# A mixture-of-experts block whose weights stream through a ring: another order of the experts, one slot more

## What is computed

```
def expert_ffn(xb, w1, b1, w2, b2):
    z = xb @ w1 + b1                                   # w1: 1024 x 2048
    x_glu = jnp.minimum(z[..., ::2], SWIGLU_LIMIT)
    x_lin = jnp.clip(z[..., 1::2], -SWIGLU_LIMIT, SWIGLU_LIMIT)
    act = x_glu * jax.nn.sigmoid(SWIGLU_ALPHA * x_glu) * (x_lin + 1.0)
    return act @ w2 + b2                               # w2: 1024 x 1024

    logits = (ht @ router_w + router_b).astype(jnp.float32)
    top_vals, top_idx = lax.top_k(logits, TOP_K)       # 4 of 32
    gates = jax.nn.softmax(top_vals, axis=-1)
    ...                                                # every token through its 4 experts
    x  = x + gate2 * MoE_top4_of_32(h2)
```

## Time and profile before

| | us |
|---|---|
| runs of the kernel before | 1756.4, 1764.86, 1767.21 |
| their median | 1764.86 |
| the profiled execution | 1758.43 |
| its span, first to last instruction | 1756.7 |

### The profile page before, as it was taken

One profiled execution on the slowest core, in us unless ns is written; L12 is line 12 of the kernel. 1 busy time (PEld: TensorE's weight loads), 2 busy tenths in 40 slices (PEclk: granted clock), 3 DMA queues, 4 the chain that ended last, 5 costly groups with the idle time before them and its releaser, 6 DMA issues.

```text
span 1756.7 us, 48721 instructions
## 1 busy us (share of the span) xinstructions
PE 1481.8 (84%) x19899; PEld 832.5 (47%) x19899; DVE 776.8 (44%) x1872; ACT 302.8 (17%) x844; POOL 530.6 (30%) x532
## 2 busy tenths in 40 slices
PE   4899998689648999999898998988978978986781
PEld 2356554364335555555554545554544534542340
DVE  4857365453365444444443433433433423422225
ACT  4121265342101111111111111110101100100000
POOL 3085999108002323222232222222211212211110
PEclk9997999899868999998999999998988988987885
DMA  9442224763761704478869999999999999999997
GB/s 270 151 49 48 86 47 98 261 200 107 299 254 43 309 20 164 163 291 322 344 269 403 358 407 368 354 408 408 408 408 408 408 408 408 408 409 409 408 408 295
DMA packets 141907, 495.58 MB, mean 282 GB/s; under 512 B 20216, under 2 KB 24580, under 8 KB 137744
## 3 DMA queue, kind: packets, MB, share of 16 engines
q1 hardware_dynamic: 128960, 469.60, 70.9%
q0 software_dynamic: 8416, 19.33, 3.1%
q10 hardware_dynamic: 4432, 5.25, 0.9%
HBM read 474.18 MB, written 17.84 MB: 280 GB/s over the span
## 4 chain that ended last, share of the span: by engine, by line
PE 53%; DMA 22%; SPq 15%; DVE 5%; issue 2%; ACT 2%; POOL 0%; ACTq 0%; POOLq 0%; DVEq 0%
PE bank L1789 30%; DMA w_ring<-mlp_w 17%; SPq L422 14%; PE bank L1506 5%; PE bank L1669 3%; PE bank L1594 2%; DMA ada_slab<-ada_w 2%; PE bank L1498 2%; DMA ada_half<-ada_w 2%; PE bank L1808 1%; PE bank L1781 1%; PE bank L1603 1%; PE bank L1769 1%; DVE final_acc L1421 1%; PE bank L1698 1%
## 5 line engine op out<-in xcount | busy, mean ns | idle before, releaser
L1789 PE MATMUL bank<-w_ring,xs_T 128*32 128x256 f32 x10240 | 620.9, 394 | 67.7 <-DMA w_ring<-mlp_w 67.5
L1789 PEld LDWEIGHTS bank<-w_ring,xs_T 128*32 128x32 f32 x10240 | 330.0, 113 | 319.9 <-DMA w_ring<-mlp_w 108.6
L643 POOL DMA_INDIRECT xs<-h_rows,row_idx x82 | 189.3, 2309 | 847.7 <-DVE row_idx L1349 817.4
L1789 PE MATMUL bank<-w_ring,act_T 128*32 128x256 f32 x5120 | 338.2, 402 | 56.1 <-DMA w_ring<-mlp_w 55.9
L1789 PEld LDWEIGHTS bank<-w_ring,act_T 128*32 128x32 f32 x5120 | 154.3, 114 | 175.3 <-DMA w_ring<-mlp_w 55.7
L1367 DVE TENSOR_SCALAR glu<-bank 128x128 f32<-128x128 f32 x160 | 46.6, 291 | 402.9 <-PE bank L1789 402.9
L945 DVE TENSOR_TENSOR slot_onehot<-iota_slots,slots 128x2048 bf16<-128x2048 f32 x83 | 189.3, 2281 | 0.0
L922 ACT ACTIVATE sigmoid<-glu 128x128 f32<-128x128 f32 x160 | 48.9, 306 | 536.2 <-DVE glu L1367 466.9
L926 ACT ACTIVATE act_T<-bank 128x128 f32<-128x128 f32 x160 | 44.3, 277 | 518.1 <-PE bank L1808 518.1
L664 POOL DMA_INDIRECT ys_rows<-y_rows_sb,row_idx x80 | 82.3, 1029 | 144.2 <-DVE y_rows_sb L945 141.9
L1344 DVE TENSOR_REDUCE row_idx_f<-bank 128x1 f32<-128x2 f32 x82 | 13.0, 159 | 209.0 <-PE bank L1769 209.0
(11 more groups left out here) (336 smaller groups left out, 1534.6 us busy)
## 6 DMA issues: line engine op xcount, KB each, us to landing
w_ring<-mlp_w SPq DMA_DIRECT2D x384, 1024.0 KB
ada_half<-ada_w SPq DMA_DIRECT2D x16, 1024.0 KB, 5.0
dense_ring<-w_in SPq DMA_DIRECT2D x4, 2048.0 KB, 14.6
final_rows<-ys_rows SPq DMA_DIRECT2D x4, 2048.0 KB, 14.4
dense_ring<-ada_w SPq DMA_DIRECT2D x3, 2048.0 KB, 29.3
w_out<-w_out SPq DMA_DIRECT2D x2, 2048.0 KB, 10.6
x_all<-x SPq DMA_DIRECT2D x2, 1024.0 KB, 14.3
ada_slab<-ada_w SPq DMA_DIRECT2D x1, 2048.0 KB, 40.3
```

Of the source, the lines that this page charges most:

```text
L643: pool.indirect_dma_start(out=xs[:], out_offset=None, in_=h2_v, in_offset=bass.IndirectOffsetOnAxis(ap=idx[:, 0:1], axis=0), bounds_check= ...
L1789: last = mm(bk[BLK * j:BLK * j + BLK, 0:ZW], x(h0 + i), w[:, i, ZW * j:ZW * j + ZW], start=False, stop=(stop and i == 1))
```

## The change

```
+FIXED = 1
-SLOTS_KIB = (132, 140, 64, 72, ..., 48, 56, 148)
+SLOTS_KIB = (132, 140, 64, 72, ..., 48, 56, 148, 120)
...
             sp.wait_ge(s["x1_ready"], NT)
+            sp.wait_ge(s["blocks_ready"], 1)
+            expert = sp.value_load(eat[0:1, 1:2], min_val=0, max_val=E - 1)
             for n in range(12, 16):
-                chunk(n)
+                chunk(n, expert)
             sp.wait_ge(s["h2_tr"], NT)
             sp.wait_ge(s["h2_ready"], NT)
-            for j in range(TILES):
-                sp.dma_start(g2q[BLK * j:BLK * j + BLK], dram["mod_rows"][0, 3 * D + ZW * j:3 * D + ZW * j + ZW]
-                             .partition_broadcast(BLK)).then_inc(s["mod_loaded"], 16)
...
             for n in range(16, 21):
-                chunk(n)
+                chunk(n, expert)
             sp.wait_ge(s["blocks_ready"], 3)
+            for j in range(TILES):
+                sp.dma_start(g2q[BLK * j:BLK * j + BLK], dram["mod_rows"][0, 3 * D + ZW * j:3 * D + ZW * j + ZW]
+                             .partition_broadcast(BLK)).then_inc(s["mod_loaded"], 16)
             for n in range(21, SLOTS):
-                chunk(n)
-            expert = None
+                chunk(n, expert)
...
-                ch(tt(cmp, bc(R[7][:, 2:E], 1, n, [P, n, n]), bc(R[7][:, 2:E], 2, n, [P, n, n]), ALU.is_gt))
+                ch(tt(cmp, bc(R[7][:, FIXED:E], 1, n, [P, n, n]), bc(R[7][:, FIXED:E], 2, n, [P, n, n]), ALU.is_lt))
...
-                ch(tt(posn[:, 2:E], posn[:, 2:E], R[6][:, 2:E], ALU.min))
+                ch(tt(posn[:, FIXED:E], posn[:, FIXED:E], R[6][:, FIXED:E], ALU.min))
+                ch(tt(ordm[:], bc(posn[:], 1, E, [P, E, E]), bc(iotaE[:], 2, E, [P, E, E]), ALU.is_equal))
+                ch(tt(lessm[:], ordm[:], bc(iotaE[:], 1, E, [P, E, E]), ALU.mult))
+                ch(dve.tensor_reduce(eatf[:], lessm[:], AX.X, ALU.add))
+                dve.tensor_copy(eat[:], eatf[:]).then_inc(s["blocks_ready"], 1)
...
-            act.wait_ge(s["blocks_ready"], 2)
+            act.wait_ge(s["blocks_ready"], 3)
...
-            pe.wait_ge(s["blocks_ready"], 2)
+            pe.wait_ge(s["blocks_ready"], 3)
```

More of the change, by code:

```diff
@@ L63 @@
 W1P = 8
[L64 removed]
+SLOTS_KIB = (132, 140, 64, 72, 32, 40, 0, 8, 16, 24, 172, 180, 80, 88, 156, 164, 96, 104, 112, 48, 56, 148, 120)
 SLOTS = len(SLOTS_KIB)
@@ L210, in program @@
         rw = pack("router_w", [P, KT, E])
+        tri = pack("tri", [P, P], BF16)
+        onb = pack("ones_bf", [P, P], BF16)
+        ones = pack("ones", [P, P])
         rb = pack("router_b", [P, E])
@@ L243, in program @@
         lessm = at("order_less", 196, [P, E, E], BF16)
-        lin = at("lin", 120, [P, 2, GW])
-        actT = at("act_T", 121, [P, 2, AH, P])
-        glu = at("glu", 122, [P, 2, GW])
-        sg = at("sigmoid", 123, [P, 2, GW])
-        g2q = at("gate2_quarters", 124, [P, ZW])
+        lin = at("lin", 197, [P, 2, GW])
+        actT = at("act_T", 128, [P, 2, AH, P])
+        glu = at("glu", K0 + 0.5 + 0.0625, [P, 2, GW])
+        sg = at("sigmoid", K0 + 1.5 + 0.0625, [P, 2, GW])
+        g2q = at("gate2_quarters", 129, [P, ZW])
         bsrc = at("b_src", 172, [96, 3072])
@@ L256, in program @@
         xT = at("xs_T", 203, [P, XH, P])
-        iotab = at("iota_slots", K0 + 2.25, [P, P])
+        iotab = at("iota_slots", K0 + 2.75, [P, P])
         fing = at("final_rows", 0, [P, 16, D])
-        fx1 = at("final_x1", 172, [P, NT, D])
+        fx1 = at("final_x1", 96, [P, NT, D])
         facc = at("final_acc", 80, [P, NT, D])
@@ L459, in _ @@
                     last_block = sp.value_load(nbi[0:1, E + e:E + e + 1], min_val=0, max_val=MAXB - 1)
-                if n >= 2 * CPE and n % CPE == 0:
+                if n % CPE == 0:
                     expert = sp.value_load(eat[0:1, n // CPE:n // CPE + 1], min_val=0, max_val=E - 1)
@@ L1229, in order_positions @@
                 dve.wait_ge(s["part_mm"], 1)
-                n = E - 2
+                n = E - FIXED
                 ch(dve.tensor_scalar(R[6], bank[7][:, 6 * E:7 * E], float(E), None, ALU.mult))
@@ L1233, in order_positions @@
                 cmp = lessm[:, 0:n, 0:n]
[L1234 to L1239 removed]
+                ch(tt(cmp, bc(R[7][:, FIXED:E], 1, n, [P, n, n]), bc(R[7][:, FIXED:E], 2, n, [P, n, n]), ALU.is_lt))
+                ch(dve.tensor_reduce(R[5][:, FIXED:E], cmp, AX.X, ALU.add))
+                ch.free(dve.tensor_scalar(posn[:, FIXED:E], R[5][:, FIXED:E], 2.0, float(FIXED), ALU.mult, ALU.add))
+                ch(dve.tensor_scalar(R[6][:, FIXED:E], R[5][:, FIXED:E], -2.0, 2.0 * E - 1.0 - FIXED, ALU.mult, ALU.add))
+                ch.free(dve.tensor_copy(posn[:, 0:FIXED], iotaE[:, 0:FIXED]))
+                ch(tt(posn[:, FIXED:E], posn[:, FIXED:E], R[6][:, FIXED:E], ALU.min))
[3 more added lines that the diff above has]
+                dve.tensor_copy(eat[:], eatf[:]).then_inc(s["blocks_ready"], 1)
             def order_matrices():
[L1243 to L1244 removed]
+                ch(tt(lessm[:], bc(posn[:], 1, E, [P, E, E]), bc(posn[:], 2, E, [P, E, E]), ALU.is_lt))
             dve.wait_ge(s["norm_router_loaded"], 64)
@@ L1313, in _ @@
             dve.tensor_reduce(dslot[:], prod[:], AX.X, ALU.add).then_inc(s["blocks_ready"], 1)
-            dve.wait_ge(s["blocks_ready"], 1)
+            dve.wait_ge(s["blocks_ready"], 2)
             dve.wait_ge(s["bias_ready"], 2)
@@ L1319, in block_ends @@
                 ch.free(tt(R[2], R[4], R[0], ALU.add))
-                ch.free(tt(lessm[:], ordm[:], bc(iotaE[:], 1, E, [P, E, E]), ALU.mult))
                 ch.sync()
@@ L1481, in _ @@
                 last = tr(bank[1][:, q * DG:(q + 1) * DG], quad[:, q].rearrange("p a b -> p (a b)"), ident[0:DG, 0:DG])
-            last.then_inc(s["af_psum"], 1)
+            last.then_inc(s["pe_prep"], 1)
             early_ada(2)
```

23 lines of the change are left out of this document (5 added, 18 removed).

## The result

The changed kernel takes 1748.72 us (median of 16 runs, 1738.71 to 1757.32) where the kernel before takes 1764.76 (median of 16, 1756.4 to 1768.44). The ratio is 0.9909 [0.9887, 0.9931]: 16 us or 0.9% less. The forecast was 27.3 us less (1737.5), with a range of 1720 to 1756. So the sign was right and the size 11 us short; by the bound of 1% the change lies just inside "within 1%", the outcome to which the prediction had given 0.18.

What follows compares the result with a forecast made beforehand. PE bounds the early large-expert blocks, the weight stream the later part. Against before, the six (3,1) pairs begin 26.0 us later, take 2.6 less, and 50.8 less follows: −27.3 from 1764.86 gives 1737.5 us, range 1720 to 1756.

Steps and rivals of the forecast that it cites:

- the start: From the order to the first block: later count and a gather slowed beside chunks make it 3.0 us late, bounds 0.5 to 5.
- the seven stalls: Seven pairs of a large and a one-block expert, positions 2 to 15: 5.7 us of stall each, 39.6 together.
- the six (3,1) pairs: Pairs of a three-block and a one-block expert at the stream's pace, one chunk further ahead: 375.6 us, before 378.2.
- The failed step: Large expert's first block: the extra slot makes its last chunk thirteenth, not fourteenth, of the run; stall 8.2 to 5.7 us.
- the rival: Stalled blocks: shorter waits keep PE's clock up, seven stalls lose 0.9 us more, −6.4, total 1731; chance 0.12.
- The gate row's cover: Before DVE's first gating: the row, queued behind chunk 20, lands at 540 to 541, 1.5 to 2.5 us ahead of need.
- The rival of a dearer gate row: At the start: the gather or gate row costs up to another 5 us, total 1743; chance 0.05.
- The chunks 12 to 22: Weight chunks issued late at the start: landed by 546, needed near 588, so no cost, with a cover of 40 us.
- The order: After 4 + 1 blocks, pairs (9,1), (6,1), (5,1) twice, (4,1) three times; block 49 ends position 15, scattered at 1182.8.
- The last four positions: Positions 28 to 31, blocks (2,1), (2,2): 121.9 us to the last expert's first block, 14 for its second.
- That the stall does not shrink: Seven pairs: the extra slot is eaten, each keeps 8.2 us; price 18 us, total 1755.5; chance 0.12.
- "Slower" by a slow restart: Pairs from position 2: slow stream restart makes stalls grow; no gain at 9.6 us, 1% slower at 12.2, about 1783; chance 0.03.

Runs made afterwards that it cites:

- x1: The changed kernel with 22 slots, without its new slot, all else as changed: 1761.01 us, ratio 0.9965 to the kernel before.
- the four traces: Profiles with 23 slots and the same pairs: the changed kernel, after again, x3 and x5; mean of the seven stalls 48.4 us.
- x7: The changed kernel with 21 slots, its last read of `x1` waiting for the last expert: 1777.26 us, ratio 1.008 to the kernel before.
- before again: The kernel before, unedited, measured and profiled a second time: 1766.46 us, ratio 1.0007 to the kernel before.
- after again: The changed kernel, unedited, measured and profiled a second time: 1749.39 us, ratio 0.9912 to the kernel before.
- x2: The changed kernel with experts ranked from the largest again, 23 slots: 1762.99 us, ratio 0.999 to the kernel before.
- x3: The changed kernel with chunks 12 to 22 all issued behind the gate row: 1746.14 us, ratio 0.9892 to the kernel before.
- x5: The changed kernel with ranks 14 and 15 exchanged, so a one-block expert is last: 1741.26 us, ratio 0.9877 to the kernel before.
- x4: The changed kernel with the next expert's register loaded ahead of SP's wait for the release: 1744.95 us, ratio 0.9894 to the kernel before.
- x6: The changed kernel with the edits of x3, x4 and x5 together: 1728.86 us, ratio 0.9801 to the kernel before.
- x8: The changed kernel with first-matrix chunks of 128 whole 8 KiB rows, products wrongly paired: 1731.06 us, ratio 0.9813 to the kernel before.
- x11: The changed kernel with the edits of x10, x3, x4 and x5 together: 1712.44 us, ratio 0.9693 to the kernel before.
- x10: The changed kernel with whole-row chunks and PE's order changed so the products are right: 1729.48 us, ratio 0.9776 to the kernel before.

## Why the forecast was 11 us short

Against the forecast, counted from the order on (1694.3 − 509.8 = 1184.5 for the last scatter), the trace has 1201.2: 16.7 us are missing. They are 1.3 of the start, 10.9 of the seven stalls and 4.5 of the six (3,1) pairs.

**The failed step** is "With 23 slots it is the thirteenth. One chunk is 1.049 MB / 408 GB/s = 2.57 us, so the stall becomes 8.2 − 2.6 = 5.7 us." The mechanism holds: the stall ends with the last chunk, that chunk is one place earlier in the run, and each slot shortens it. The size doesn't hold. 408 GB/s is the pace of a running stream, and the chunk that the slot saves stood at the restart, where the place it frees is taken by the slow first chunk of the next expert: 1.7 us of 2.57 arrive by the landings, and 1.4 by PE's use of the last chunk (table below). The base was right: x1, which has the new order with 22 slots, has 58.1 / 7 = 8.3 us a pair. The mean with 23 slots is 6.9, not 5.7. So of the 10.9 us the slot's size makes 18.0 − 9.7 = 8.3 (the prediction's 7 × 2.57 for the 9.7 that x1 and the four traces show), and this trace lies 2.1 above the mean of its four. One pair's end in PE's rows: the start of the previous large expert's last block and the last 16 matmuls, before and after.

```profile
837.84 0.29 PE L1781 MATMUL bank<-b_cat,expert_sel 96*32 96x256 bf16 x4
...
880.65 1.07 PE L1789 MATMUL bank<-w_ring,act_T 128*32 128x256 f32 x16 [1.40 <-DMA w_ring<-mlp_w]
```
```profile
807.42 0.29 PE L1782 MATMUL bank<-b_cat,expert_sel 96*32 96x256 bf16 x4
...
849.03 1.94 PE L1790 MATMUL bank<-w_ring,act_T 128*32 128x256 f32 x16 [1.40 <-DMA w_ring<-mlp_w]
...
850.95 4.01 PE L1790 MATMUL bank<-w_ring,xs_T 128*32 128x256 f32 x64
```

The last chunk is used 42.8 us after that start before, and 41.6 after: 1.2 us for the slot. Its matmuls take 1.94 us in this pair where they took 1.07, but over all pairs that isn't so. The same two times from PE's rows, means of six pairs:

| kernel | last chunk used, us after that start | from its use to the next block, us |
|---|---|---|
| 21 slots (x7) | 45.6 | 1.31 |
| 22 slots (before, before again, x1) | 43.1, 43.2, 43.2 | 1.40, 1.48, 1.52 |
| 23 slots (after, after again, x2, x3) | 41.9, 41.8, 41.7, 41.9 | 1.43, 1.63, 1.42, 1.47 |
| 23 slots, last single (x5) | 41.5 | 1.16 |
| 23, preload (x4, x6) | 41.1, 41.1 | 1.51, 1.47 |
| 23, whole rows (x8) | 40.1 | 1.37 |

**The clock.** In the changed kernel's stalled block the granted clock (first of the last three numbers) is 0.79 where PE waits and 0.83 behind it, between the levels of 1.2 and 2.4 GHz:

```profile
846.00:850.00 4.00, 2.04 (x28) 1.01 (x32) 2.92 (x5) 0.00 (x0) 2.52 (x2) 0.79 1.03 410
850.00:855.00 5.00, 5.00 (x88) 2.72 (x84) 0.51 (x2) 0.00 (x0) 1.03 (x1) 0.83 1.02 404
```

The time from the last chunk's use to the next block is 0.89 us in pairs where the granted clock there is 1.00, and 1.71 where it is 0.50; so the clock can be worth 0.8 us a pair. Two pairs, (5,4) of the changed kernel and of x5, from the last chunk's landing on:

```profile
1009.20:1013.10 3.90, 3.37 (x36) 1.25 (x32) 2.17 (x4) 0.00 (x0) 2.52 (x2) 0.50 1.02 405
```
```profile
1008.00:1010.70 2.70, 1.31 (x28) 0.57 (x24) 1.64 (x4) 0.00 (x0) 2.35 (x2) 1.00 1.03 411
```

Both levels occur in every kernel, and with 22 slots and with 23 the means are alike (1.40 to 1.52, and 1.42 to 1.63). So the clock took nothing from the slot, and it didn't give what the rival had put on it, 6.4 us for a clock that stays up. It is a part of the spread between traces: x5's seven stalls are 5.0 us shorter than after's, and its seven times from use to next block 1.6 us shorter in sum (8.7 for 10.3), since four of them are at 0.89 and only two of after's. The Trainium skill (TensorE: Matmul & The Clock Gate, "HAM oscillation — how this bites in real kernels") would have shorter waits keep the clock up. These traces can't test that: the stall is shorter with 23 slots, but the single waits in it are not (1.40 us ahead of the last chunk in both rows above). What sets the clock in these blocks stays open.

**The start.** The gather was slowed as forecast: 7.7 us to its turn, for 7.1, and ACT's copy behind it begins 26.1 us after the order for 23.0 before, the 3.0 of the forecast. The gate row's cover wasn't there. It was to land right behind the ninth chunk, 25 us after the chunks were issued; 524.6 + 25 is 550, and DVE got it at 555.5. So the term "cost 0" was wrong, and its price is the 1.3 us by which the start is later than its 3.0. The rival of a dearer gate row was the right place with too large a price.

**The chunks 12 to 22** cost nothing, and x3 shows it with a still later issue.

**The order** was right to the block, and its worth too: the forecast had 27.3 + 3.0 − 20.8 (the slot's, eight times 2.6) = 9.5 us for it, and the traces show 7.9.

**The six (3,1) pairs** were to take 375.6 us, by a stream that is a chunk ahead. They take 380.0, as in x1 with 22 slots (379.4), and 378.2 before. The extra slot shows no gain there: that is 2.6 of the 4.5 us. The likeliest reason, which no run tests, is that the chunk was already counted in the stall ahead of the first pair. The other 1.9 are over the 378.2 of before; x1 has 1.2 of them without the slot and x5 0.1 with it, so they are little more than the spread.

**The last four positions** were forecast at 121.9 + 14 = 135.9 us and took 136.0. That it meets so well is luck in part: the first block of position 31 came after 120.7 us and its second took 15.3, two misses of 1.3 that cancel.

**The rivals.** That the stall does not shrink had 0.12. It shrank by about half of what was forecast, and the reason given for the rival, register loads of SP between the releases, is worth about 0.5 us a pair by x4 and x6. "Slower" by a slow restart had the mechanism that I now hold for the larger part of the missing gain; at 6.9 us a pair it is far from the 9.6 at which it decides. (Its bound for 1% slower should read 5.7 + (27.3 + 17.6) / 7 = 12.1, not 12.2.)

**The times.** The traces show 10.6 us less for the expert part, the medians of 16 runs 16. The other 5 or so must lie ahead of the order or in what one profiled execution doesn't show; the order is done 509.8 to 521.3 us into the span, for the same code. They weren't located. The forecast was also made against a trace whose dense part was the fastest of all 14 (509.8), which moved nothing, since only its differences were used.

**What stays open**: why the first chunk of the next expert comes slowly. The register load is worth 0.4 us of it (9.8 for 10.2), whole rows 0.9 (9.3). One chunk's pace behind 6.0 would be 8.7, so that half a microsecond or more has no cause shown. The two together (x11) land the second chunk at 9.3 and the last at 38.2, no earlier than whole rows alone, so the two parts don't add. In x10 and x11 the second chunk comes only 2.9 and 2.8 us behind the first, but there the first is half a microsecond later.
